# Expert outputs added up by the scatter, two rows per token at the end, and attention's first units on other banks

## The reference

```python
# first block, after its token mixer and a layer norm: h is [512, 1024]
scores = sigmoid(h @ router_w)                      # 64 experts
idx = top_k(masked scores + router_b, 8)            # 8 experts for each token
wts = scores[idx] / sum(scores[idx]) * 2.5
for each expert e, for the tokens that chose it:    # at most 128 rows in a block
    hid = silu(h[tok] @ w1[e]) * (h[tok] @ w3[e])   # [rows, 256]
    routed[tok] += wts * (hid @ w2[e])              # [rows, 1024]
f = routed + (silu(h @ sw1) * (h @ sw3)) @ sw2      # the shared expert
x = layernorm(ALPHA * x + g2 * f) * ln2_w + ln2_b

# second block, for each of two layers
proj = rms_norm(x) @ w_in                           # queries, keys, values; rope on queries and keys
attention: plain heads over the keys that an index picks (256 at most), and differential heads
x = x + mixed @ w_out ; x = x + (silu(gate) * up) @ w_down
```

## Time and profile before

| | us |
|---|---|
| median of 3 runs (2882.22 to 2887.02) | 2884.3 |
| the profiled execution | 2883.77 |
| its span in the trace | 2882.0 |
| TensorE busy, of the span | 2727.0 (95%) |
| VectorE busy | 1718.6 (60%) |
| ScalarE busy | 1161.9 (40%) |
| GpSimd busy | 215.3 (7%) |

### The profile page before, as it was taken

How to read it: one execution, slowest core, us unless ns; L and a number is a source line. 1 busy time by engine, 2 the same in 40 slices (tenths; PEclk the granted TensorE clock), 3 DMA queues, 4 the chain that set the end, 5 groups by cost and what they waited for, 6 DMA issues and landing times.

```text
span 2882.0 us, 42287 instructions
## 1 busy us (share of the span) xinstructions
PE 2727.0 (95%) x17110; PEld 2099.5 (73%) x17110; DVE 1718.6 (60%) x3109; ACT 1161.9 (40%) x2102; POOL 215.3 (7%) x212
## 2 busy tenths in 40 slices
PE   6998998889999999999988999999999998999998
PEld 6887767774766776666646766888888775788887
DVE  5256876666677777777646786432334688433333
ACT  3323553221365555565513338322223327432232
POOL 0000000000022122222200120000000030000000
PEclk9998998999999999999999989999999999999999
DMA  6210002424488989999975330324224240223321
GB/s 236 88 59 23 1 3 76 123 62 167 156 319 337 348 346 358 352 361 349 356 293 185 95 89 9 120 70 139 73 81 131 92 110 12 89 87 95 117 67 65
DMA packets 186543, 442.40 MB, mean 154 GB/s; under 512 B 21283, under 2 KB 110694, under 8 KB 167014
## 3 DMA queue, kind: packets, MB, share of 16 engines
q1 hardware_dynamic: 161862, 396.59, 38.3%
q0 software_dynamic: 24480, 43.04, 5.0%
HBM read 426.43 MB, written 38.29 MB: 161 GB/s over the span
## 4 chain that ended last, share of the span: by engine, by line
PE 80%; DVE 9%; DMA 5%; ACT 4%; issue 2%; SPq 0%; POOL 0%; ACTq 0%; DVEq 0%; POOLq 0%
PE ps L296 19%; PE ps L297 19%; PE ps L298 19%; PE ps L2522 6%; DMA ring<-in_ew 3%; PE ps L1519 2%; PE ps L2036 2%; PE ps L2548 2%; PE ps L2761 1%; PE ps L2240 1%; DVE Pb L3508 1%; DMA yr<-y_rows 1%; DVE spA L2458 1%; PE ps L3394 1%; PE ps L1854 1%
## 5 line engine op out<-in xcount | busy, mean ns | idle before, releaser
L2973 DVE TENSOR_TENSOR wf<-ring,wf 128x1024 fp32r<-128x1024 f32 (+1 forms) x152 | 181.6, 1196 | 312.0 <-ACT wf L2969 311.7
L2969 ACT ACTIVATE wf<-ring 128x1024 fp32r<-128x1024 f32 (+1 forms) x152 | 156.8, 1033 | 347.6 <-PE ps L298 347.6
L296 PE MATMUL ps<-hxh,wf 128*128 128x512 f32 (+1 forms) x736 | 279.9, 380 | 2.3 <-DVE hxl L3136 2.3
L297 PE MATMUL ps<-hxl,wf 128*128 128x512 f32 (+1 forms) x736 | 279.5, 380 | 0.0
L298 PE MATMUL ps<-hxh,wf 128*128 128x512 f32 (+1 forms) x736 | 279.5, 380 | 0.0
L2458 DVE TENSOR_TENSOR spA<-ring,spA 128x1024 fp32r<-128x1024 f32 x156 | 184.5, 1221 | 101.0 <-ACT spA L2453 100.8
L2522 PE MATMUL ps<-ring,hdT 128*128 128x512 f32 x520 | 234.8, 594 | 0.8 <-issue 0.8
L2453 ACT ACTIVATE spA<-ring 128x1024 fp32r<-128x1024 f32 x156 | 157.7, 1054 | 51.8 <-DMA ring<-in_ew 43.9
L2458 DVE TENSOR_TENSOR spB<-ring,spB 128x1024 fp32r<-128x1024 f32 x104 | 124.1, 1221 | 67.6 <-ACT spB L2453 64.9
L2522 PEld LDWEIGHTS ps<-ring,hdT 128*128 128x128 f32 x520 | 93.8, 190 | 94.3 <-issue 91.1
L296 PEld LDWEIGHTS ps<-hxh,wf 128*128 128x128 f32 x736 | 138.4, 188 | 28.9 <-DVE hxl L3136 2.8
(11 more groups left out here) (623 smaller groups left out, 6135.7 us busy)
## 6 DMA issues: line engine op xcount, KB each, us to landing
ring<-in_ew SPq DMA_DIRECT2D x65, 2048.0 KB, 12.1
ring<-in_ew SPq DMA_DIRECT2D x65, 1024.0 KB
ring<-in_w_in SPq DMA_DIRECT2D x17, 2048.0 KB, 8.0
ring<-in_w_gate SPq DMA_DIRECT2D x20, 1024.0 KB, 5.6
ring<-in_w_up SPq DMA_DIRECT2D x20, 1024.0 KB, 8.1
ring<-in_w_down SPq DMA_DIRECT2D x16, 1024.0 KB, 5.1
adaw<-in_ada_w SPq DMA_DIRECT2D x24, 512.0 KB, 6.5
ring<-in_w_out SPq DMA_DIRECT2D x6, 2048.0 KB, 8.2
```

Of the source, the lines that this page charges most:

```text
L296: pe.matmul(o, lhs[0], rhs[0], start=start, stop=False)
L297: pe.matmul(o, lhs[0], rhs[1], start=False, stop=False)
L2969: act.activation(item_part(n)[0], item_raw(n), ACT.Copy).then_inc(*w_hi.inc(n))
L2973: v.tensor_tensor(item_part(n)[1], item_raw(n), f(item_part(n)[0]), ALU.subtract).then_inc(*w_lo.inc(n))
```

## The change

**Weights by slot.** `val` gets six columns instead of four: tile, token in the tile, 1, and the token's weight for this expert in three bf16 parts (`weight_parts`, four VectorE instructions, called twice). It is filled in the list stage instead of in the router's. `match_pe` carries all six columns, for group 0 in two passes (the weights in a pass of their own, "w"). `slot_weights` adds the three parts into `wsl`, one weight for each slot: three small VectorE instructions for each group. The expert's hidden rows are multiplied by it in the instruction that makes `hd2`. `jr`, `j8`, `w8`, `dg` and what made them are gone.

**Accumulating scatter.** `y_rows` has 1024 rows: two arrays of one row for each token. Expert blocks with even numbers go into the first and odd ones into the second. GpSimd clears it at the start with one DMA of 4 MB (a row of zeros of `hg`, eight times), and every scatter has `compute_op=ALU.add`. Scatter n waits on GpSimd's queue until scatter n-2 has landed, and the gather that follows it in the queue waits with it.

**Combine.** SP loads 8 pieces of 512 KB, and TensorE makes six products with the identity for each tile: two for `fac`, four for the two rows. `sums` and `diag_dve` are gone, and so are the waits of the second block's third weight load for the buffers of the combine.

**Attention's banks.** Even units use banks 2 and 3, odd ones 0 and 1. Unit 0 waits for no copy, unit 1 for the last copy alone, and the wait for the two last rope DMAs moves to unit 16, the first plain one. `zb` is placed elsewhere and cleared before the last rope instructions.

```diff
-    yD = nc.dram_tensor("y_rows", (4096, D), F32, kind="Internal").ap()
+    yD = nc.dram_tensor("y_rows", (1024, D), F32, kind="Internal").ap()
...
     def match_pe(pe, g, bank):
-        pe.wait_ge(*l_dve.val(("P", g)))
-        for n in range(8 * g, 8 * g + 8):
+        lo, hi = (0, 3) if g == 0 else (3, 6) if g == "w" else (0, 6)
+        pe.wait_ge(*l_dve.val("w" if g == "w" else ("P", g)))
+        at = 0 if g == "w" else 8 * g
+        for n in range(8):
             for i in range(4):
-                m = pe.matmul(bank[:, 4 * (n % 8):4 * (n % 8) + 4], Pm[:, i, n - 8 * g, :], val[:, i, n, :], start=(i == 0), stop=(i == 3))
+                m = pe.matmul(bank[:, 6 * n + lo:6 * n + hi], Pm[:, i, n, :], val[:, i, at + n, lo:hi], start=(i == 0), stop=(i == 3))
...
-        v.tensor_copy(val[:, :, 64:96, 2], ps[4][:, 128:256].rearrange("p (i e) -> p i e", i=4)).then_inc(*l_dve.inc("val"))
+        weight_parts(v, slice(64, 96), ps[4][:, 128:256].rearrange("p (i e) -> p i e", i=4), wov[:, :, :]).then_inc(*l_dve.inc("val"))
...
+    def weight_parts(v, cols, w, left):
+        v.wait_ge(*V.val())
+        v.tensor_copy(val[:, :, cols, 3], w).then_inc(*V.inc())
+        v.wait_ge(*V.val())
+        v.tensor_tensor(left, w, val[:, :, cols, 3], ALU.subtract).then_inc(*V.inc())
+        v.wait_ge(*V.val())
+        v.tensor_copy(val[:, :, cols, 4], left).then_inc(*V.inc())
+        v.wait_ge(*V.val())
+        return v.tensor_tensor(val[:, :, cols, 5], left, val[:, :, cols, 4], ALU.subtract)
...
+    def slot_weights(v, g, bank):
+        v.wait_ge(*l_pe.val(("P", g) if g else "Pw"))
+        v.wait_ge(*V.val())
+        v.tensor_copy(cvi[:, :, 3:6], bank[:, 0:48].rearrange("p (b c) -> p b c", c=6)[:, :, 3:6]).then_inc(*V.inc())
+        v.wait_ge(*V.val())
+        v.tensor_tensor(cvi[:, :, 4], cvi[:, :, 4], cvi[:, :, 5], ALU.add).then_inc(*V.inc())
+        v.wait_ge(*V.val())
+        v.tensor_tensor(wsl[:, 8 * g:8 * g + 8], cvi[:, :, 3], cvi[:, :, 4], ALU.add).then_inc(*l_dve.inc(("ws", g)))
...
     def scatter(g, n, b):
         return g.indirect_dma_start(out=yD, out_offset=bass.IndirectOffsetOnAxis(ap=idx[:, n, 1:2], axis=0), in_=yb[:, b, :],
-                                    in_offset=None, bounds_check=4095, oob_is_err=False)
+                                    in_offset=None, bounds_check=1023, oob_is_err=False, compute_op=ALU.add)
...
         g.memset(hg[:, :, :], 0.0).then_inc(*g_hg.inc("set"))
         g.wait_ge(*g_hg.val("set"))
+        g.dma_start(yD.rearrange("(a p) d -> p a d", p=128), bcm(hg[:, 2, :], 8)).then_inc(*d_zero.inc("in"))
...
+                g.wait_ge(*(d_sca.val(n - 2) if n >= 2 else d_zero.val("in")))
                 scatter(g, n, n % 3).then_inc(*d_sca.inc(n))
...
-                v.tensor_tensor(hd2[:, n % 2, :], sl[:, n % 2, :], ps[2 + n % 2][:, 256:512], ALU.mult).then_inc(*k_dve.inc(("hd2", n)))
+                v.wait_ge(*l_dve.val(("ws", n // 8)))
+                v.scalar_tensor_tensor(out=hd2[:, n % 2, :], in0=sl[:, n % 2, :], scalar=wsl[:, n:n + 1], in1=ps[2 + n % 2][:, 256:512],
+                                       op0=ALU.mult, op1=ALU.mult).then_inc(*k_dve.inc(("hd2", n)))
...
-        for n in range(16):
-            i, k = divmod(n, 4)
-            if n >= 6:
-                sp.wait_ge(*pair_done(n - 6))
-            sp.dma_start(yrow(n), yv[i, :, 2 * PAIRS[k]:2 * PAIRS[k] + 2, :]).then_inc(*d_yr.inc(n))
+        for n in range(8):
+            if n == 6:
+                sp.wait_ge(*t_pe.val(0))
+            sp.dma_start(yr[:, n // 2, n % 2, :], yv[n % 2, n // 2]).then_inc(*d_yr.inc(n))
...
+            for hf in range(2):
+                pe.matmul(b[hf][:, :], ident, fac[:, i, hf * 512:(hf + 1) * 512], start=True, stop=False)
+            for a in range(2):
+                pe.wait_ge(*d_yr.val(2 * i + a))
+                for hf in range(2):
+                    m = pe.matmul(b[hf][:, :], ident, yr[:, i, a, hf * 512:(hf + 1) * 512], start=False, stop=(a == 1))
+            m.then_inc(*t_pe.inc(i))
...
             if u >= 2:
                 pe.wait_ge(*u_max.val((l, u - 2)))
-            else:
+            elif u == 1:
                 pe.wait_ge(*p_r.val((l, 18)))
-                if u:
-                    for c in (17, 18):
-                        pe.wait_ge(*rope_done(l, c))
+            if u == 16:
+                for c in (17, 18):
+                    pe.wait_ge(*rope_done(l, c))
```

More of the change, by code:

```diff
@@ L2207, in _program @@
     rk = sb("rk", [128, 4, 96], c=m4)
-    jr = sb("jr", [128, 4, 64], c=m4)
-    j8 = sb("j8", [128, 8, 64], c=m4)
+    wsl = sb("wsl", [128, 96], c=m4)
+    val = sb("val", [128, 4, 96, 6], BF, c=m4)
     m4.close()
@@ L2335, in list_dve @@
         weights_dve(v)
+        weight_parts(v, slice(0, 64), wtok[:, :, :], sel[:, :, :]).then_inc(*l_dve.inc("w"))
         index_list(v, 0, ps[7])
@@ L2347, in list_dve @@
         v.tensor_tensor(hid[:, 1, :], gsl[:, 1, :], ps[3][:, :], ALU.mult).then_inc(*h_dve.inc(1))
+        slot_weights(v, 0, ps[4][:, 256:304])
         v.wait_ge(*l_pe.val("tri"))
@@ L2410, in list_part @@
             match_dve(v, g, i)
-        elif 44 <= n < 56:
-            slot_weights(v, (n - 44) // 3, (n - 44) % 3)
     NE = 64
@@ L2504, in expert_pool @@
                     g.wait_ge(*k_pe.val(("t1", n - 3)))
+                if n == 2:
+                    g.wait_ge(*d_zero.val("in"))
                 gather(g, n, n % 3).then_inc(*d_gat.inc(n))
@@ L2628, in over_pool @@
         g.wait_ge(*l_dve.val(("idx", 11)))
+        for k in (NX - 2, NX - 1):
+            g.wait_ge(*d_sca.val(k))
         g.wait_ge(*k_pe.val(("t1", NX - 1)))
@@ L2713, in _program @@
     b1.close()
-    PAIRS = (0, 3, 1, 2)
-    d_yr = Loads([sem(f"d_yr{k}") for k in range(6)], [1] * 16)
-    ring_rows = ring[:, 8192:12288].rearrange("p (a b d) -> p a b d", a=2, b=2)
-    def yrow(n):
-        return yr[:, n % 6, :, :] if n % 6 < 4 else ring_rows[:, n % 6 - 4, :, :]
-    def pair_done(n):
-        i, k = divmod(n, 4)
-        return t_sum.val(i) if k == 1 else t_pe.val((i, k))
+    d_yr = Loads([sem(f"d_yr{k}") for k in range(6)], [1] * 8)
     d_ln2 = Signal(sem("d_rows"), ["in"], 32)
-    t_dg = Signal(sem("combine_diag"), ["set"])
-    t_sum = Signal(sem("combined"), range(4))
-    t_pe = Signal(sem("combine_mm"), [(i, k) for i in range(4) for k in (0, 2, 3, "all")])
+    t_pe = Signal(sem("combine_mm"), range(4))
     t_var = Signal(sem("ln_var"), range(4))
@@ L2783, in combine_act @@
         norm_hi(act, 0, 0, 3)
-    def diag_dve(v):
-        v.wait_ge(*h_act.val((3, 1)))
-        for i in range(4):
-            m = v.tensor_tensor(dg[:, i, :, :], bcm(ident, 6), bc(w8[:, i, 0:6], 128), ALU.mult)
-        m.then_inc(*t_dg.inc("set"))
-    def combine_dve(v):
-        def sums(i):
-            f_ = fac[:, i, :]
-            v.wait_ge(*d_yr.val(4 * i + 1))
-            v.scalar_tensor_tensor(out=f_, in0=yrow(4 * i + 1)[:, 0, :], scalar=w8[:, i, 6:7], in1=f_, op0=ALU.mult, op1=ALU.add).then_inc(*V.inc())
-            v.wait_ge(*V.val())
-            v.scalar_tensor_tensor(out=f_, in0=yrow(4 * i + 1)[:, 1, :], scalar=w8[:, i, 7:8], in1=f_, op0=ALU.mult,
-                                   op1=ALU.add).then_inc(*t_sum.inc(i))
+    def combine_dve(v):
         def tokens(i, between):
             f_, x = fac[:, i, :], xt[:, i, :]
-            v.wait_ge(*t_pe.val((i, "all")))
+            v.wait_ge(*t_pe.val(i))
             if i == 0:
@@ L3361, in lproj_dve @@
             elif p >= 12:
+                if p == 27:
+                    v.wait_ge(*w_use.val(n0 + 25))
+                    v.memset(zb[:, :], 0.0).then_inc(*V.inc())
+                    v.wait_ge(*V.val())
+                    v.memset(zb[0:64, 448:512], -1e30).then_inc(*V.inc())
                 rope_part(p - 9)
```

90 lines of the change are left out of this document (29 added, 61 removed).

## The result

The changed kernel takes 2912.6 us (median of 4 runs, 2908.8 to 2917.2) against 2884.3 before: ratio 1.0098, interval 1.0081 to 1.0116, so about 28 us slower. The forecast was 2880, its range 2862 to 2901.

The account below looks back on a forecast made before the run. TensorE, with DMA engines almost as full, was taken to bound the expert stage. Expert stage +20, experts' start +2, combine -20 and attention -5.6 sum to -3.6 us, so 2880 us was forecast, range 2862 to 2901.

Parts of the forecast that it names:

- I take a share of 0.94: Expert stage: DMA engines, busy 537 of 600 us, would fill to 0.94 with adding's 46 us more, costing +20 us.
- The price of adding a row: Expert stage: from rope's accumulating DMAs, adding costs 54 us of engine time per MB more, 0.79 us a step.
- The idle time: Expert stage, 860 to 1460 us: 63 us of DMA idle time could hold the adding's extra 46 us.
- 51 us, if each microsecond is paid: Expert stage: upper bound of adding's cost, since loads are issued only on TensorE's progress and must land in time.
- Rival B: Expert stage: adding paid in full, by share saturation or a bandwidth cap; +38 there gives 2898 us; chance 0.22.
- Rival A: Expert stage: adding hidden in the engines' idle time, TensorE's waits growing at most 5 us; 2863 us; chance 0.20.
- Rival C: Combine: gain partly lost, 5 us by TensorE's clock returning late and 3 by late ln2 rows; 2887 us; chance 0.08.
- The wait of scatter n for n-2: Expert stage, GpSimd's queue: costs nothing, as that scatter was issued 20.7 us before and lands in 10.5.
- The start of the experts: Before the first expert: `weight_parts` +1.1 us, group 1's list +0.6, filling `val` mostly hidden; +2 us (1 to 4).
- The combine: Last scatter to projection: VectorE sets the pace, 39.5 us to a projection start at 1518.7; -20 us (-24 to -14).
- Attention: Units 0 and 1: no rope DMA wait and earlier `zb` clearing save 2.8 us a layer; -5.6 us (0 to -7).
- the signs named: Profile after: DMA share 0.94 or more, step near 10.7 us, landings 13 to 14, projection 49 to 50 after last scatter.

Follow-up runs that it names:

- e14: Changed kernel with live slots dealt evenly over the 16 DMA engines (even order) and GpSimd instead of VectorE filling `val`: 2863.8 us, ratio 0.9924.
- e11: Kernel before with a second plain scatter each step, 64 rows from slots 64 to 127 into an array nobody reads: 2890.1 us, ratio 1.0019.
- e13: Changed kernel with the even order of slots alone, each DMA engine getting every 16th rank: 2864.1 us, ratio 0.9919.
- e1: Changed kernel with a scatter that overwrites instead of adding, all else kept: 2862.6 us, ratio 0.992.
- e15: Changed kernel with the even order, GpSimd filling `val`, and each 2 MB load ahead of the previous expert's 1 MB load: 2856.0 us, ratio 0.9892.
- e9: Changed kernel with another order of slots, rank r in slot 79 r mod 128: 2872.5 us, ratio 0.9959.
- e12: Changed kernel with slots spread over groups of 8 neighbours, GpSimd filling `val`, and 2 MB loads ahead of 1 MB loads: 2886.9 us, ratio 1.001.
- e4: Kernel before with the attention part of the change alone: 2877.7 us, ratio 0.9972.
- e16: Kernel before with the even order of slots and the attention part of the change: 2874.1 us, ratio 0.9959.

## Why the prediction was wrong

The step that failed is "I take a share of 0.94": the expert stage at +20, where it took +45. The share was taken of 16 engines together, while the eight engines that serve the full slots had almost no idle time. The term's parts, one by one:

- *The price of adding a row* was too high, not too low. Rope's rows gave 0.79 us of all engines a step; the rows in HBM took 328 - 159 = 169 ns more each, 56.6 x 169 / 16 = 0.60. The multiple itself held: 328 / 159 is 2.06, and 2.1 was taken from rope.
- *The idle time* was not there. The 63 idle us were a mean over 16 engines, and the row can't show that half of them did most of GpSimd's work (by e14's count and the rule, 82% of the rows in all 65 steps, and all of them in the 40 steps with up to 64 rows). For an engine with 8 live rows a step is, by estimate from the packets' medians, 8 x (611 + 309 + 159 + 159) ns = 9.9 us before, against TensorE's 10.14 in a step without list work, and 8 x (611 + 309 + 159 + 328) = 11.3 after, against a measured step of 725.0 / 65 = 11.15 (packets overlap by some 5 to 20 ns). By this estimate TensorE was the bound by 0.2 us a step, not by a tenth of the step. The upper end, "51 us, if each microsecond is paid", held the value; the reason given for it did not.
- *Rival B* had the size (+38) and the sign, but its mechanisms, a share that saturates at 0.92 and a cap of 350 GB/s, are both refuted by e11 (1.00 and 382 GB/s) and e13. The 358 GB/s that the rival quotes from the Trainium skill do not bind this core, which runs alone. The Trainium skill says so itself elsewhere (Perfetto Trace Analysis, the note "HBM >100% is normal for single-core trn2 kernels"), and these runs agree with that note. Rival A's "hidden" came true only with the even order, in e13. Rival C's late clock did not: the projection's first 5.4 us ran at a granted clock of 0.67, against 0.50 before.
- *The wait of scatter n for n-2* costs nothing, as forecast: the last scatter goes out 0.80 us after ScalarE's last copy of rows, as before (0.83). But it lands in 6.2 us in place of 3.7, where 1 more was put in (0 to 2). In e1, without adding, it is 3.3. The packets say where the 2.5 us lie: the first row starts 2.12 us after the issue in place of 1.57, and the last one ends at 5.86 in place of 3.34, so about 0.5 is the adding's later start and 2.0 are its rows' longer time on the eight engines. In the even order the rows end at 3.9 to 4.0, and the scatter lands in 4.5 and 4.4 us (e14, e15). e13, in the same order, took 5.9, because its first row started only at 3.59; e9's did so at 3.46, and no run shows why.
- *The start of the experts*, +2 (1 to 4), measured +4.1. Half of it lies behind the overflow list: from its `rk` to the first expert's rows VectorE needs 9.5 us (783.72 to 793.23) in place of 7.5, near the 1.7 forecast. The other half lies ahead of it and was to be mostly hidden. There `weight_parts` is called a first time, which the sum leaves out (2.5 us, 765.90 to 768.43), and the nine small instructions that fill `val`, put at 1.3 us, lasted 5.1 (753.5 to 758.6), two of them beside GpSimd's clearing at 2.8 and 2.5 us. With the filling on GpSimd (e12, e14, e15) the part is still 40.5, 3.1 above before, so the filling is about 1 us of the 4.1 (and up to 2.7, since the same code took 43.2 in other executions). The trace of before had the same thing in view, though not in the rows I took: its `rk` instruction beside that clearing took 2.16 us (from 749.81), and 0.41 after.
- *The combine* was right in its main term: from VectorE's first instruction (1536.08) to the projection 39.5 us passed, as forecast. The 49.8 us from landing to projection ("49 to 50" among the signs, 47.9 by the sum's own terms) owe something to luck: the rows came 4.09 us after the wait began and not 6.7, but VectorE had to wait for all four products of the tile (recorded as x8), 6.05 us at a mean granted clock of 0.60, where two at 0.84 were put in. With the last scatter's 2.5 us the part gave -16.8, within -24 to -14.
- *Attention* was right in kind: VectorE's distance from the last rope instruction to unit 1's maximum went from 6.05 to 3.02 us in each layer, 3.0 less, against 2.8 forecast. The whole is -7.2 in e4 against -5.6.
- *The clearing DMA* was not seen to cost anything; no run took it away, so that stays untested.

Of the signs named, DMA share 0.94 and a mean step of 10.7 failed in the first view one would open: 0.90 and 11.2. The landings, forecast at 13 to 14 us, took 15.4. The "17 MB more" of reading for the adding shows nowhere: the page counts 413.85 MB read against 426.43, 12.6 less, just the rows that the combine no longer loads. If the destination is read, it shows in the packets' time alone.

## What to carry to other kernels

A DMA share is a mean over engines; a landing is set by the fullest. Before counting a tenth of idle share as room, ask how many rows each engine gets, above all where an indirect DMA skips rows, and look at a transfer that runs alone: a share of 0.5 there means half of the engines. Where slots have no order of their own, deal the live ones over the engines first; here the order was worth 49 us to the adding kernel and some 4, not clear of the noise, to the plain one (e16 against e4).

Price a DMA change per row on the fullest engine, up to 8 rows here, and compare with the bound engine's step: 9.9 against 10.14 leaves 0.2 us, whatever the mean share says.

## What the runs showed of the hardware

- An adding 4 KB row into HBM takes 328 ns of a DMA engine, a plain one 159.
- Rows left out of an indirect DMA cost their engine next to nothing (packets of 4 and 8 bytes, 7 to 24 ns), so the live rows decide its load.
- The first row of an adding scatter starts 2.11 us after its issue at the earliest, that of a plain one 1.52 to 1.57 (the last scatter of each kernel).
- One core alone moved 382 GB/s over 100 us with all engines full (e11).
- A small VectorE instruction that ran beside GpSimd's clearing of 12 KB a partition took 2.5 to 2.8 us in place of 0.44.
